# Latent attention in a two-block kernel: a stage per head instead of per token half, and score products of 64 rows

## The reference, cut to what matters

```
def _mla_attention(q_nope, q_rope, k_nope, k_rope, v):
    scale = 1.0 / math.sqrt(QK_HEAD_DIM)
    def block(args):                       # 128 queries at a time
        qn_b, qr_b = args
        s = (jnp.einsum("bqhd,bkhd->bhqk", qn_b, k_nope)
             + jnp.einsum("bqhr,bkr->bhqk", qr_b, k_rope)).astype(jnp.float32) * scale
        p = jax.nn.softmax(s, axis=-1).astype(v.dtype)
        return jnp.einsum("bhqk,bkhd->bqhd", p, v)
```

## Time and profile before

| | us |
|---|---|
| median of 3 runs | 2232.94 |
| lowest, highest | 2231.92, 2234.74 |
| the profiled execution | 2233.09 |
| its span in the trace | 2231.2 |

### The profile page before, as it was taken

One profiled execution on the slowest core, in us unless ns is written; L12 is line 12 of the kernel. 1 busy time (PEld: TensorE's weight loads), 2 busy tenths in 40 slices (PEclk: granted clock), 3 DMA queues, 4 the chain that ended last, 5 costly groups with the idle time before them and its releaser, 6 DMA issues.

```text
span 2231.2 us, 26898 instructions
## 1 busy us (share of the span) xinstructions
PE 2194.5 (98%) x10449; PEld 1832.1 (82%) x10449; DVE 1513.4 (68%) x1967; ACT 1110.8 (50%) x1516; POOL 46.0 (2%) x68
## 2 busy tenths in 40 slices
PE   9999999999999999999999999998999999999997
PEld 7888888888888888888888888887888887788886
DVE  6675468768876777777777778766465566555566
ACT  6575456444445444444433444565465454546542
POOL 1000000100000000000000000000000000000000
PEclk9999999999999999999999999999999999999999
DMA  7544655499795889998989988573464582554573
GB/s 260 186 127 129 186 179 163 143 373 309 262 331 188 297 298 308 307 308 302 304 302 306 311 301 299 181 238 95 142 194 137 161 279 81 165 166 147 159 234 117
DMA packets 242607, 500.61 MB, mean 224 GB/s; under 512 B 17008, under 2 KB 26144, under 8 KB 241328
## 3 DMA queue, kind: packets, MB, share of 16 engines
q1 hardware_dynamic: 239088, 484.08, 66.4%
q0 software_dynamic: 3392, 14.82, 1.9%
HBM read 496.70 MB, written 2.12 MB: 224 GB/s over the span
## 4 chain that ended last, share of the span: by engine, by line
PE 91%; DVE 3%; ACT 3%; issue 1%; DMA 1%; POOL 0%; SPq 0%; POOLq 0%; ACTq 0%; DVEq 0%
PE bank L898 88%; PE bank L901 3%; DVE wl L1866 1%; ACT arena L1312 1%; ACT wh L1312 1%; DMA raw<-in_w_in 1%; DVE arena L1874 0%; DVE arena L1873 0%; DVE arena L1869 0%; DMA raw<-in_w_ple_gate 0%; ACT hh L1312 0%; DVE arena L1866 0%; ACT L1312 0%; DVE hl L1866 0%; POOL st L749 0%
## 5 line engine op out<-in xcount | busy, mean ns | idle before, releaser
L1312 ACT ACTIVATE wh<-raw 128x1024 fp32r<-128x1024 f32 (+2 forms) x500 | 520.0, 1042 | 664.3 <-PE bank L898 621.6
L1866 DVE TENSOR_TENSOR wl<-raw,wh 128x1024 fp32r<-128x1024 f32 (+2 forms) x500 | 599.5, 1201 | 325.6 <-ACT wh L1312 323.6
L898 PE MATMUL bank<-wh,hh 128*128 128x512 f32 (+1 forms) x1568 | 619.9, 396 | 9.4 <-DVE hl L1866 5.2
L898 PE MATMUL bank<-wl,hh 128*128 128x512 f32 (+1 forms) x1568 | 605.5, 387 | 0.0
L898 PE MATMUL bank<-wh,hl 128*128 128x512 f32 (+1 forms) x1568 | 605.3, 387 | 0.0
L898 PE MATMUL bank<-wh,ah 128*128 128x512 f32 (+1 forms) x1168 | 456.1, 391 | 2.4 <-ACT arena L1312 1.7
L898 PE MATMUL bank<-wh,al 128*128 128x512 f32 (+1 forms) x1168 | 450.9, 387 | 0.0
L898 PE MATMUL bank<-wl,ah 128*128 128x512 f32 (+1 forms) x1168 | 450.2, 386 | 0.0
L898 PEld LDWEIGHTS bank<-wh,hh 128*128 128x128 f32 x1568 | 295.4, 189 | 69.0 <-issue 9.8
L898 PEld LDWEIGHTS bank<-wh,hl 128*128 128x128 f32 x1568 | 294.5, 188 | 60.6
L898 PEld LDWEIGHTS bank<-wl,hh 128*128 128x128 f32 x1568 | 296.0, 189 | 55.3
(11 more groups left out here) (132 smaller groups left out, 1356.5 us busy)
## 6 DMA issues: line engine op xcount, KB each, us to landing
raw<-in_w_in SPq DMA_DIRECT2D x245, 512.0 KB, 3.7
arena<-in_w_ada SPq DMA_DIRECT2D x148, 384.0 KB, 4.9
arena<-in_w_gate_up SPq DMA_DIRECT2D x97, 512.0 KB, 4.5
raw<-in_w_ada SPq DMA_DIRECT2D x108, 384.0 KB, 4.8
raw<-in_w_out SPq DMA_DIRECT2D x80, 512.0 KB, 5.0
raw<-in_w_gate_up SPq DMA_DIRECT2D x79, 512.0 KB, 4.6
raw<-in_w_down SPq DMA_DIRECT2D x45, 512.0 KB, 5.2
arena<-in_w_down SPq DMA_DIRECT2D x43, 512.0 KB, 5.2
```

Of the source, the lines that this page charges most:

```text
L898: return i.matmul(o, l, x, start=start, stop=stop, skip_group_check=False)
L1312: return i.activation(o, x, fn, scale=scale, **k)
L1866: return i.tensor_tensor(o, a, b, op)
```

## The change

A stage is now (z, j): one head, 2j+z, and both token halves. Both stages of a j start in the same slot (`kvb` 1 + 8, four slots after the old start of half 0, one after that of half 1). Stage z=0 issues the scores of both heads, into two banks, one for each head: plain products of token half 0 for both heads, then the four rotated products, then the plain ones of half 1. A rotated product takes only the 64 rows of its head (`QR[64w:64w+64]` with the same rows of `KR`), so `KR` is one tile, copied whole, without zeros. The two semaphores go up with the last two products. Transposes, copies, value products and the scaled result are done by head, and stand for z=0 and z=1 directly behind each other.

```
-        start(done(f"kvb{l}", 1) + 4, "mla", l, 0)
-        start(done(f"kvb{l}", 1) + 7, "mla", l, 1)
+        for z in range(2):
+            start(done(f"kvb{l}", 1) + 8, "mla", l, z)
...
-        KR = [kb(24, 1), kb(11, 1)]
+        KR = kb(24, 1)
...
-                    bk = bank(("ms", l, half, j), S.a_mla, l, half, j)
-                    for z in range(2):
-                        o = bk[:, z * 256:(z + 1) * 256]
-                        mm(o, QN[:, 2 * j + z, ms], KN[:, 2 * j + z, :], True, False)
-                        t = mm(o, QR[:, j, ms], KR[z], False, True)
-                    t.then_inc(*S.p_mla.up(l, half, j, "s"))
...
+                    if z == 0:
...
+                        two_banks = [bank(("ms", l, w, j), S.a_mla, l, w, j) for w in range(2)]
+                        o = [[bk[:, m * 256:(m + 1) * 256] for bk in two_banks] for m in range(2)]
...
+                        def straight(m):
+                            return [mm(o[m][w], QN[:, 2 * j + w, m * P:(m + 1) * P], KN[:, 2 * j + w, :], m == 0, m == 1)
+                                    for w in range(2)]
...
+                        def rotated(m):
+                            for w in range(2):
+                                rows = slice(64 * w, 64 * w + 64)
+                                mm(o[m][w], QR[rows, j, m * P:(m + 1) * P], KR[rows, :], m == 1, m == 0)
...
+                        straight(0)
+                        rotated(0)
+                        rotated(1)
+                        t = straight(1)
+                        for w in range(2):
+                            t[w].then_inc(*S.p_mla.up(l, w, j, "s"))
...
-                e.wait_ge(*S.v_ckv.at(l, "z"))
-                ps = BANK[bank_of["kr", l]]
-                copy(KR[0][0:64, :], ps[0:64, 0:256])
-                copy(KR[1][64:P, :], ps[64:P, 0:256]).then_inc(*S.a_kr.up(l))
+                copy(KR, BANK[bank_of["kr", l]][:, 0:256]).then_inc(*S.a_kr.up(l))
...
-                i.memset(KR[0][64:P, :], 0.0)
-                i.memset(KR[1][0:64, :], 0.0).then_inc(*S.v_ckv.up(l, "z"))
```

More of the change, by code:

```diff
@@ L639, in hg_stat, with mla_stat @@
             return ST[:, 56 + 16 * b + 8 * k:56 + 16 * b + 8 * k + 8]
-        def mla_stat(half, j, k):
-            o = 166 + 12 * half + 6 * (j % 2) + 2 * k
+        def mla_stat(z, j, k):
+            o = 166 + 12 * z + 6 * (j % 2) + 2 * k
             return ST[:, o:o + 2]
@@ L1271, in mla @@
                     yield
-                    e.wait_ge(*S.a_mla.at(l, half, j))
-                    bk = bank(("mt", l, half, j), S.v_mla, l, half, j, "c")
-                    for z in range(2):
+                    e.wait_ge(*S.a_mla.at(l, z, j))
+                    bk = bank(("mt", l, z, j), S.v_mla, l, z, j, "c")
+                    for m in range(2):
                         for k in range(2):
-                            t = tr(bk[:, (2 * z + k) * P:(2 * z + k + 1) * P], PB[half][:, z, k * P:(k + 1) * P])
-                    t.then_inc(*S.p_mla.up(l, half, j, "t"))
+                            t = tr(bk[:, (2 * m + k) * P:(2 * m + k + 1) * P], PB[z][:, m, k * P:(k + 1) * P])
+                    t.then_inc(*S.p_mla.up(l, z, j, "t"))
                     yield
                     yield
-                    e.wait_ge(*S.v_mla.at(l, half, j, "c"))
-                    bk = bank(("mo", l, half, j), S.v_mla, l, half, j, "o")
-                    for z in range(2):
+                    e.wait_ge(*S.v_mla.at(l, z, j, "c"))
+                    bk = bank(("mo", l, z, j), S.v_mla, l, z, j, "o")
+                    h = 2 * j + z
+                    for m in range(2):
                         for k in range(2):
-                            h = 2 * j + z
-                            t = mm(bk[:, z * P:(z + 1) * P], pt[:, (2 * z + k) * P:(2 * z + k + 1) * P],
+                            t = mm(bk[:, m * P:(m + 1) * P], pt[:, (2 * m + k) * P:(2 * m + k + 1) * P],
                                    VN[:, k, h * P:(h + 1) * P], k == 0, k == 1)
-                    t.then_inc(*S.p_mla.up(l, half, j, "o"))
+                    t.then_inc(*S.p_mla.up(l, z, j, "o"))
                     yield
@@ L1806, in kvb, with mla @@
                 copy(KN[:, 2 * j:2 * j + 2, :].rearrange("p h t -> p (h t)"), BANK[bank_of["kn", l, j]][:, :]).then_inc(*S.a_kvb.up(l, j))
-            def mla(l, half):
+            def mla(l, z):
                 for j in range(4):
                     yield
[L1811 to L1816, removed]
+                    nm, sm = mla_stat(z, j, 0), mla_stat(z, j, 1)
+                    e.wait_ge(*S.v_mla.at(l, z, j, "nm"))
+                    ps = BANK[bank_of["ms", l, z, j]][:, :].rearrange("p (m k) -> p m k", m=2)
+                    for m in range(2):
+                        x = f(PB[z][:, m, :], ps[:, m, :], ACTF.Exp, scale=SCL, bias=nm[:, m:m + 1], accum=sm[:, m:m + 1])
+                    x.then_inc(*S.a_mla.up(l, z, j))
                     yield
@@ L2489, in qb, with mla @@
                 x.then_inc(*S.v_qb.up(l, j))
-            def mla(l, half):
+            def mla(l, z):
                 for j in range(4):
-                    key = (l, half, j)
-                    nm, sm, rs = (mla_stat(half, j, k) for k in range(3))
+                    key = (l, z, j)
+                    nm, sm, rs = (mla_stat(z, j, k) for k in range(3))
                     e.wait_ge(*S.p_mla.at(*key, "s"))
-                    ps = BANK[bank_of[("ms", *key)]][:, :].rearrange("p (h k) -> p h k", h=2)
+                    ps = BANK[bank_of[("ms", *key)]][:, :].rearrange("p (m k) -> p m k", m=2)
                     then(red(nm, ps, ALU.max, negate=True), S.v_mla, *key, "mx")
```

17 lines of the change are left out of this document (8 added, 9 removed).

## The result

The changed kernel takes 2225.31 us (median of 6 runs, 2223.63 to 2226.45) against 2232.0 us before (6 runs, 2231.46 to 2234.74): a ratio of 0.9968 with a 95% interval of 0.9958 to 0.9977, so 6.7 us or 0.32% less. It is the time of rival (a), 2226.4, within 1.1 us. The profiled execution of the changed kernel took 2224.22 us, with a span of 2222.4.

A forecast was written before the change was run, and what follows sets the result against it. PE was taken to bound the kernel (91% of the chain that ended last). Rotated products -1.9 us and gaps -2.9 us sum to -4.8 us, so 2228.2 us (chance 0.43), range 2225.5 to 2234.5.

The forecast's parts named there:

- rival (a): Rotated products in the scores: full overlap, four steps; -6.5 us with the gaps gone, 2226.4 us; chance 0.18.
- start to start distances: On PE, an edit counts only if it changes the distance between two matmuls' starts; 0.215 us per 256-column scores matmul.
- five steps: Rotated products in the scores: PE starts in order, so the eight 64-row matmuls half overlap and take 1.08 us.
- The products' term: Attention scores: a j costs 3.21 us instead of 3.44, -0.23 us in each of 8 j, -1.9 us.
- The visit: PE in the scores: changing to 64 rows and back costs 0.41 us, once in each of 8 j.
- The gaps: Attention of both layers: PE's 0.28 us wait at transposes and 1.15 us wait at scores go, -2.9 us.
- The timeline: ACT and DVE around the zf transposes: ah ends at 1.7 us, al 2.4, copies 3.8, first scaled result 9.1.
- The air: At the next scores: DVE's first result at 9.1 us, its bank wanted by PE at 11.2, 2 us to spare.
- No new waits: Third slot behind the scores: two pairs of exponentials come in time, air of 1.4 us at least; 0 us.
- (c): Rival: the gaps stay or move, as DVE and ACT do two stages' work in one slot; about 2230.5 us; chance 0.20.
- (d): Rival: ACT bounds the transposes in the third slot behind the scores; 2236 to 2237 us with old gaps back; chance 0.07.

The follow-up runs named there:

- by_head: Changed kernel with the four rotated products ordered head by head, both token halves of the first head, then of the second; 2227.23 us, ratio 0.9974.
- two_visits: Changed kernel with plain, rotated, plain, rotated products, so PE changes to 64 rows and back twice in a j; 2229.39 us, ratio 0.9985.
- same_rows: Changed kernel with rows 0 to 63 in all four rotated products, leaving out part of the second head's scores; 2234.49 us, ratio 1.0002.
- slots_only: Kernel before with only the slots changed, both halves starting at kvb 1 + 8, 128-row rotated products kept; 2230.62 us, ratio 0.9991.
- zf_first: Kernel before with ACT serving the second zf block's stage first in its slots; 2229.78 us, ratio 0.9984.
- early: Changed kernel with both stages of a j one slot earlier (kvb 1 + 7); 2230.62 us, ratio 0.999.
- after_again: Changed kernel run a second time, nothing edited; 2227.1 us, ratio 0.9972.
- att_both: Changed kernel with both halves of the first block's attention starting in slot 35 instead of 32 and 35; 2235.09 us, ratio 1.0005.
- att_long: Changed kernel, both first-block attention halves from slot 32, one more slot between scores and transposes, each half issuing its own scores; 2240.28 us, ratio 1.0031.
- att_pair: Changed kernel, both first-block attention halves from slot 32, one more slot before transposes, half 0 issuing both halves' scores alternately; 2236.35 us, ratio 1.0014.

## Why the prediction was right or wrong

**What bounds the kernel, and start to start distances: right.** What each edit changed was found again as a distance between matmuls.

**The step that failed: five steps for four pairs of matmuls.** The prediction said that PE starts in order, "A1, then A2 with B1, B2 with C1, C2 with D1, D2, which is five steps, 1.08 us". The records show four pairs, so A1 with B1, A2 with B2: four steps, 0.86 us. The sum of steps and visit thus is 1.72 + 0.86 + 0.40 = 2.98 us (2.99 measured) and not 3.21, 0.22 us in each of 8 j, 1.8 us in all. That is nearly all of the 1.9 us by which the gain was larger than forecast, and it is rival (a), which I had given 0.18 on the ground that the queue's order spoke against it. by_head shows that this order doesn't bind PE: another order gave the same block to the hundredth.

**The products' term.** Forecast -1.9 us (8 x 0.23 are 1.84), measured 6.81 - 3.03 = 3.78 us.

**The visit: right.** 0.41 us from one place of the trace; 0.40 inside the block, 0.37 from two_visits. Without other rows it costs all that the slots bring (same_rows).

**The gaps: right, size and cause.** Forecast -2.9 us, slots_only 3.03, zf_first 3.20. The timeline behind it, counted from the end of the last unit before the `zf` transposes, 1698.86 in the changed kernel, was off in its middle. ACT and DVE of the changed kernel:
```profile
1700.12 1.08 ACT L1324 ACTIVATE wh<-raw 128x1024 fp32r<-128x1024 f32 x1
1701.07 0.62 ACT L1324 ACTIVATE ah<-bank 128x512 fp32r<-128x512 f32 x1
```
```profile
1701.73 0.69 DVE L1875 TENSOR_TENSOR al<-bank,ah 128x512 fp32r<-128x512 f32 x1 [1.08 <-ACT ah L1324]
1702.33 1.28 DVE L2512 COPY arena<-bank 128x512 f32<-128x512 f32 x2
...
1708.15 0.75 DVE L1875 TENSOR_TENSOR arena<-bank,st 128x256 f32<-128x256 f32 x2
```
`ah` ends at 2.8 us (1.7 forecast: two scalings of ACT stand ahead of the weight copy), `al` at 3.6 (2.4), the copies at 4.7 (3.8), the first result near 9.7 (9.1). PE wants it at 11.6 (11.2). The air was forecast as 2 us and is 1.9, since both ends moved. What I had not counted: the twelve transposes take 1.45 us where 0.43 + 0.86 = 1.29 were counted. The totals don't show these 0.16 us: slots_only gave 3.03 us where 2.9 were forecast.

**No new waits: right for this slot.** (c) and (d) did not come. early shows that (d) was no idle fear: one slot earlier ACT gives back 4.8 us.

**The range.** It reached one us below (a), 2225.5, and the time was 0.2 us lower. The sum for (a) was 2232.94 - 6.5; the attention gave 6.8 and the median of six runs lies 1.1 us beside 2226.4. Of the 2.9 us between the forecast of 2228.2 and the time, 0.9 are not the change's at all: the kernel before had 2232.94 when I forecast and 2232.0 beside the changed kernel. after_again, the same kernel, has 2227.1, inside the range, so that the time fell outside by so little is chance, and the step above is wrong either way. With the 1.7 and 3.4 us that the clock of the earlier trace rows costs, the end beyond a rival of 0.18 should have had two us of room and not one.

**Open.** Whether the four places are a fixed number: in all four 64-row blocks of att_both and of att_long four matmuls start alone, the ninth of the program starts beside the fifth, and the first half's last signal is on the eleventh record, though the steps are 0.11 us in two of the blocks (128 columns) and 0.215 in the other two. So it looks like a count and not a time, but no run changed what stands between. Whether both halves could write into one bank: here they never did. And how ACT's 5.75 us in att_pair could be avoided: ACT works there from 170.14 to 178.94 us without a gap, on eight exponentials, two table loads of 1.28 us and its evictions, and no run took one of these away.

## What to carry to other kernels

A float32 product that uses 64 rows cost as much as one of 128 rows unless there were as many of the other half beside it, into another bank; then two ran in the time of one. Going there and back costs 0.4 us, so that a visit with two products of 256 columns gains nothing worth having and one with four gains 0.46 us. Before stages are moved for such a gain, read the queues of the other engines at the hand-overs: here the order of a table load, two exponentials and one copy on ACT was worth 3.2 us, one slot earlier costs 4.8 us. And where the whole time scatters by some us for reasons outside, compare the distance between the same two matmuls: it repeats to a few hundredths of a us.

## What the runs showed of the hardware

- 64-row matmuls of different row halves start 7 ns apart (13 to 14 in the order head by head) and run at once, four pairs in four steps of 0.215 us, though each float32 product is two matmuls; matmuls of the same half never do (same_rows). With eight of one half first, the first matmul of the other starts beside the fifth and not sooner, and sixteen take 2.89 us (att_both) against 1.92 when they alternate (att_pair).
- A change between 128 and 64 rows makes two distances about 0.1 us longer on either side, 0.37 to 0.41 us for both changes, the same in the first block, in the attention and in two_visits.
- After a wait of 5.75 us (att_pair) PE's 512-column matmuls started 0.43 us apart instead of 0.23, with a granted clock of 0.66 from 176 to 186 us.
- ACT's table load took 1.28 us and nothing more: in the earlier trace rows the copy ahead of it ends at 1706.19, the load runs from 1706.21 to 1707.49, and the exponential starts at 1707.51.
